# The first expert product released after the first picks, and three half down units queued ahead of the ninth place

## What is computed

```python
def expert_block(args):
    toks, wb, e = args
    xb = hf[toks]
    hid = jax.nn.silu(jnp.matmul(xb, w_g[e])) * jnp.matmul(xb, w_u[e])
    return jnp.matmul(hid, w_d[e]) * wb[:, None]
```

## Time and profile before

| | |
|---|---|
| time, median of 3 runs | 1052.52 us (1051.52 to 1053.54) |
| time of the profiled execution | 1054.09 us |
| its span, first to last instruction | 1051.9 us |
| mean granted TensorE clock | 0.938 of full speed |
| PE busy | 913.0 us (87%) |
| DVE busy | 469.8 us (45%) |
| ACT busy | 345.5 us (33%) |
| read from memory | 298.84 MB |

### The profile page before, as it was taken

The page is one execution under the profiler, slowest core; times in us unless marked ns, Lnnn a source line. Parts: engine busy times, 40 slices in busy tenths (PEclk is TensorE's granted clock), DMA queues, the critical chain, the costliest instruction groups (busy, mean ns, idle before and its releaser), DMA issues.

```text
span 1051.9 us, 14155 instructions
## 1 busy us (share of the span) xinstructions
PE 913.0 (87%) x5968; PEld 661.4 (63%) x5968; DVE 469.8 (45%) x795; ACT 345.5 (33%) x557; POOL 6.1 (1%) x13
## 2 busy tenths in 40 slices
PE   6999999989889865867676775999999989999997
PEld 6969878954236421312222131388999989999986
DVE  6789869411001010010101010189766676888842
ACT  5432465211000010100000010258655745666632
POOL 0000000000000000000000000000100000000000
PEclk9999999999989987888888796999999999999999
DMA  9785332969999999999999999982434244565451
GB/s 319 273 299 205 145 120 90 409 242 426 423 407 426 409 426 425 424 429 424 428 420 429 423 427 426 406 308 82 129 132 161 81 161 160 173 210 180 163 198 40
DMA packets 78331, 301.24 MB, mean 286 GB/s; under 512 B 4035, under 2 KB 30788, under 8 KB 62658
## 3 DMA queue, kind: packets, MB, share of 16 engines
q1 hardware_dynamic: 76624, 298.83, 72.1%
q10 hardware_dynamic: 1314, 1.07, 0.4%
q0 software_dynamic: 336, 0.53, 0.3%
HBM read 298.84 MB, written 1.05 MB: 285 GB/s over the span
## 4 chain that ended last, share of the span: by engine, by line
PE 60%; DMA 28%; DVE 6%; ACT 3%; issue 1%; SPq 1%; DVEq 0%; PEldq 0%; ACTq 0%
PE bank L1406 11%; DMA ring<-in_w_gate_e_dram 9%; DMA ring<-in_w_down_e_dram 8%; DMA ring<-in_w_up_e_dram 7%; PE bank L1068 7%; PE bank L1424 6%; PE bank L682 5%; PE bank L1297 3%; PE bank L1312 3%; PE bank L773 3%; PE bank L1126 3%; PE bank L709 2%; DMA qvpr<-in_w_down_e_dram 2%; PE bank L1098 2%; PE bank L941 2%; PE bank L1201 2%
## 5 line engine op out<-in xcount | busy, mean ns | idle before, releaser
L1068 PE MATMUL bank<-ring,big 128*32 128x512 f32 x768 | 164.2, 714 | 79.2 <-DMA ring<-in_w_up_e_dram 40.3
L1068 PEld LDWEIGHTS bank<-ring,big 128*32 128x32 f32 x768 | 39.3, 127 | 196.0 <-issue 92.7
L349 DVE TENSOR_TENSOR ring_parts<-ring,ring_parts 128x2048 fp32r<-128x2048 f32 (+1 forms) x54 | 118.8, 2248 | 37.6 <-ACT ring_parts L341 37.3
L341 ACT ACTIVATE ring_parts<-ring 128x2048 fp32r<-128x2048 f32 (+1 forms) x54 | 98.5, 1874 | 54.1 <-DMA ring<-in_w_up_dram 27.0
L2244 DVE TENSOR_TENSOR xT<-bank,xT 128x512 f32<-128x512 f32 x32 | 22.1, 692 | 138.5 <-PE bank L1112 138.5
L1406 PE MATMUL bank<-mrg_parts,ring_parts 128*128 128x256 f32 x640 | 82.3, 281 | 0.0
L1406 PEld LDWEIGHTS bank<-mrg_parts,ring_parts 128*128 128x128 f32 x640 | 78.5, 189 | 0.0
L2199 DVE TENSOR_TENSOR big<-big,const 128x128 f32<-128x128 f32 x14 | 3.5, 289 | 157.9 <-PE bank L1055 157.9
L1068 PE MATMUL bank<-hs,big 128*32 128x512 f32 x128 | 67.8, 682 | 0.0
L1098 PE MATMUL bank<-ring,big 128*32 128x512 f32 x336 | 46.9, 687 | 19.1 <-DMA ring<-in_w_down_e_dram 16.3
L1068 PE MATMUL bank<-qvpr,big 128*32 128x512 f32 x112 | 60.7, 695 | 0.6 <-DMA qvpr<-in_w_gate_e_dram 0.6
(11 more groups left out here) (398 smaller groups left out, 1614.6 us busy)
## 6 DMA issues: line engine op xcount, KB each, us to landing
ring<-in_w_up_e_dram SPq DMA_DIRECT2D x24, 2048.0 KB, 28.8
ring<-in_w_gate_e_dram SPq DMA_DIRECT2D x24, 2048.0 KB, 22.3
ring<-in_w_down_e_dram SPq DMA_DIRECT2D x17, 2048.0 KB, 20.7
ring<-in_w_in_dram SPq DMA_DIRECT2D x12, 2048.0 KB, 14.1
ring<-in_w_up_dram SPq DMA_DIRECT2D x22, 1024.0 KB, 7.0
ring<-in_w_down_e_dram SPq DMA_DIRECT2D x12, 1024.0 KB, 20.6
ring<-in_w_down_dram SPq DMA_DIRECT2D x5, 2048.0 KB, 7.8
ring<-in_w_out_dram SPq DMA_DIRECT2D x4, 2048.0 KB, 9.0
```

What stands on the lines that cost most here:

```text
L341: signal(act.activation(pairs[stage][u % 3][0][:, part], raws[stage][u % 3][:, part], ACT.Copy), stage + "_hi")
L349: signal(eng.tensor_tensor(lo[:, part], raws[stage][u % 3][:, part], hi[:, part].bitcast(F32), ALU.subtract), name)
L1068: mm = pe.matmul(bank[part][CAP * j:CAP * j + CAP, :], xeT[:, c, CAP * j:CAP * j + CAP], w[j][c], start=(c == 0), stop=(c == DC - 1))
```

## The change

DVE increments `hidden` and `added` directly behind the first two picks, not behind the number of turns. As the routing scratch and `sig` share words, ACT now waits for `rounds` before it starts `expert_step`. PE no longer waits for the bank of `cnt` ahead of the first expert product; it waits for it before `late_keys`, together with the banks of `kx` 4 and 5. On SP the three first halves of the units 9, 10 and 11 are issued one behind the other, and the wait for `keys_read` with the load of the second half of the ninth place comes after all three. No arithmetic changes.

```diff
                 for i in range(3):
-                    if i == 2:
-                        sp.wait_ge(S["keys_read"], 1)
-                        load_spare(1)
                     sp.wait_ge(S["half_used"], i + 1)
                     w = w_d[0, (i + 1) // 2, (i + 1) % 2]
                     sp.dma_start(expert_slots[i][:, 0:2048], w[:, 0]).then_inc(S["down_early"], 16)
+                sp.wait_ge(S["keys_read"], 1)
+                load_spare(1)
                 sp.wait_ge(S["half_used"], 4)
...
             GATHER_BANKS = (5, 6)
-            late = [("cnt", 0)]
-            assert not any(PLACE[use][0] in GATHER_BANKS for use in late)
+            assert not PLACE[("cnt", 0)][0] in GATHER_BANKS
...
             gather(range(4))
             keys_by_chunks(4, range(6, 8))
-            for use in late:
-                copied(pe, use)
...
                     if part and first and step == 0:
-                        for m_ in (4, 5):
-                            copied(pe, ("kx", m_))
+                        for use in (("kx", 4), ("kx", 5), ("cnt", 0)):
+                            copied(pe, use)
                         late_keys()
...
                 move(("kx", m), att[:, (8 + m) * T:(9 + m) * T], T)
+            act.wait_ge(S["rounds"], 1)
...
                 dve.tensor_tensor(pick[:, t], here, iota, ALU.is_equal).then_inc(S["pick_step"], 1)
+            dve.sem_inc(S["hidden"], 1)
+            dve.sem_inc(S["added"], 1)
...
             last_turn = dve.value_load(count_i[0:1, 0:1], min_val=PAIRS - 1, max_val=PAIRS * ROUNDS - 1)
-            dve.sem_inc(S["hidden"], 1)
-            dve.sem_inc(S["added"], 1)
```

## The result

| | before | changed |
|---|---|---|
| median, 7 runs each | 1052.52 us (1051.20 to 1053.73) | 1047.54 us (1045.58 to 1049.14) |
| ratio of the two | | 0.9946, 95% interval 0.9933 to 0.9959 |
| the same, on another chip, 11 runs of the changed kernel | | 0.9966, 0.9952 to 0.9981 |
| span of the profiled execution | 1051.9 us | 1043.8 us (1044.4 in the second) |

The changed kernel is faster, by 5.0 us in the medians (5.7 us by the ratio, 4.3 to 7.1 by its interval), and by 3.6 us (2.0 to 5.1) on the other chip. The forecast was 5.3 us; the median of the first chip agrees with it, the interval of the second ends just short of it.

A forecast was written before the change was run, and what follows sets the result against it. The expert weight stream was taken to bound the kernel from 231 to 676 us. PE's 2.78 (wait) and 1.69 (clock) give 4.47 us; with the order the stream's lead is 5.3: 1052.5 - 5.3 = 1047.2 us, range 1045.2 to 1049.8.

The forecast's parts named there:

- The word: PE's first expert product, released earlier, starts at 214.05 instead of 216.83: 2.78 us of wait gone.
- the three conditions: What PE's first expert product still waits for: the picks, the rows and PE's own queue, the queue being latest.
- The clock: Without the idle time PE's clock stays up, so the first expert product takes 3.57 us, not 5.26: 1.69 us.
- The order: SP issues three halves before the `keys_read` wait, closing a stream break; the stream's lead becomes 5.3 us against PE's 4.47.
- the break closes: The weight stream's second break, at 228 to 231 us, worth 1.73 us, disappears; not all of it is kept.
- a gap of 0.8 us: New stream gap: the queue ends at 241.6, data of the up product's end trigger start at 242.4.
- "nearly closed": With 0.6 us to the first byte, the new gap would nearly vanish: lead 6.2 us, time 1046.3.
- The covers: Moved waits cost nothing: count's bank has 11.6 us of cover, ACT's `rounds` wait is early, DVE's increments some tenths at most.
- The rival on the other side: Slower: the ninth place lands about 10 us or more after issue, delaying the up product; 1054.8 us, chance 0.04.
- The passage to the end: While the weight stream sets the pace, each microsecond of earlier start is worth one at the end, unless broken anew.
- 15 us of queue: Step 1's first three units, 6.29 MB from 245.51 on; what PE frees meanwhile is issued without a break.
- the later dip at 356 us: Stream dip of 1.2 us at 356 to 364, from late memory keys; moves with the stream, plus or minus 1.2 us.

The follow-up runs named there:

- e5: Kernel before, with 6 unread matmuls of 128x256 filling PE's idle time ahead of the first expert product; ratio 0.9995 (0.9986 to 1.0004).
- e3: Changed kernel, with PE's wait for the count's bank also kept ahead of the first expert product; ratio to the kernel before 0.9967 (0.9956 to 0.9978).
- e4: Kernel before, with 24 unread matmuls of 128x256 put on PE ahead of the first expert product; ratio 1.0058 (1.0041 to 1.0075).
- e2: Kernel before, with only SP's new order of loads, the word still given late; ratio 0.9987 (0.9977 to 0.9998).
- e1: Changed kernel with SP's old order of loads, so only the early word remains; ratio to the kernel before 0.9957 (0.9944 to 0.9970).
- e6: Changed kernel, with 6 unread matmuls ahead of the first expert product to delay it without idle time; ratio to the kernel before 0.9980 (0.9971 to 0.9989).
- g2: Changed kernel with first halves as quarters, step 1's unit 0 in halves, and PE's turn-count read moved early; ratio to the kernel before 0.9952 (0.9935 to 0.9968).
- f2: Changed kernel, with unit 0 of step 1 loaded in two halves, the first at half the up product; ratio to the kernel before 0.9951 (0.9938 to 0.9964).
- g1: Changed kernel, with PE's read of the number of turns moved ahead of the memory's keys; ratio to the kernel before 0.9949 (0.9935 to 0.9964).
- f1: Changed kernel, with the three first half units split into quarters, the first quarters issued earlier; ratio to the kernel before 0.9958 (0.9945 to 0.9971).
- f3: Changed kernel with first half units as quarters and unit 0 of step 1 in two halves; ratio to the kernel before 0.9953 (0.9940 to 0.9966).

## Why the prediction was right, step by step

**The word.** Forecast 2.78 us of wait; the start moved from 3.74 to 0.96 us behind the key chunk, 2.78. That PE's own queue would be the last of the three conditions held. **The clock.** Forecast 1.69; the product took 1.70 us less, and e5 gives 1.59 at the marks with the idle time filled and nothing else changed. That it is the idle time that does it was argued from one case in the prediction; for this place e3, e4 and e5 show it (2.71 us of it: fallen; 1.00, or none: not). It isn't a rule on length: elsewhere the clock fell behind 2.40 us and held behind 2.90 (last section).

**The order.** Forecast: the break closes, a gap of 0.8 us opens behind it, 0.8 us net. Measured: gap 0.47 us, net 1.0 by bytes (e2), and 0.9 to 1.0 between e1 and the changed kernel. The first issue's data started later than in the sum: 115 and 213 GB/s at 218 to 220 put the start at 219.2, 1.73 us behind the issue and not 1.32. The shorter gap made up for it: that the two errors, 0.4 and 0.3 us, cancel is luck. The Trainium skill's 0.6 us to the first byte ("DMA: Bandwidth & Descriptors", section "Latency and other measured facts") would have given a lead of 6.2 us, as the prediction's estimate. The 1.73 us and the lead of 5.3 speak against using it for a stream here. The prediction's "nearly closed" gap takes the 0.6 us for the second restart alone; taken for both, the gap stays 0.8 us, with the same lead.

**The covers.** ACT's new wait, the count's wait ahead of the late keys and DVE's two increments cost nothing that shows: L999 starts 226.41 - 222.84 = 3.57 us behind the product, as before. The ninth place landed 2.5 us before PE asked for it, against 3.5 us in the sum. The rival on the other side had its first condition half fulfilled (7.3 us to land, where 10 would decide), and no more. The Trainium skill's rule on completion out of issue order ("DMA: Bandwidth & Descriptors", section "Queues, rings and completion order") did no harm here. Of the ninth place's 7.3 us, 2.8 are the halves still ahead of it (219.2 + 7.5 - 223.9) and 2.5 its own bytes.

**The passage to the end.** Forecast: one for one. e4 shows it over 5.9 us. But two steps were thinner than I put them. I said that within 15 us of queue what PE frees is issued without a break; behind the next trigger, at 278.86, a gap worth 0.44 us opened all the same. And I said that the later dip at 356 us moves with the stream and is good for plus or minus 1.2 us. The table shows that it decides: in eight of the thirteen rows the lead at the last mark is that of the trigger, within 0.2 us, whatever it was at the first mark (e3: 3.32, 1.81, 1.85; e6: 2.64, 0.96, 0.98). Between them lie 47 us in which PE alone sets the time, and the clock can fall in it at two places, behind the landing of the first mark and at the loop's entry. Their number gives the length of the stretch. In eight profiles the clock fell at one place, and it is 47.5 to 47.6 us. In e1 and g2 it also fell at one place, but ahead of the first product behind the landing, and it is 48.4 and 48.2. In e3, e6 and f2 it fell at both: 49.0 to 49.2. In g1 it fell at neither: 45.8. The profile before and the first one after are both of the first kind (47.52 and 47.56 us), so the 5.4 us came through; that both drew the same kind was luck too. This is a part of the spread of the runs, with the 2.4 us behind the last landing.

**Open.** Why e2, f1, f3, g1 and g2 lose 0.5 to 2.6 us between the trigger and the last mark was not settled. The landings in between narrow it down: from the one near 400 us to the one near 597 us each of these leads keeps within about 0.2 us, and 0.5 to 1.5 us of each are lost from there to the last mark (in f3 1.5 between the landings at 633 and 674 us). The rest, in f3 and g1 above all, is lost between the trigger and 400 us. No run isolates either. And the gain in time itself is known only to 2.0 to 7.1 us over both measurements, so the times can't say which of the last marks' 5.1 to 5.4 us is right, and the second measurement (3.6 us, 2.0 to 5.1) leaves open that less than the forecast reaches the end.

## What to carry to other kernels

A wait that looks like 2.7 us can be worth more: ask what the idle time does to the clock of the work behind it, and what that work releases. A lead in a stream of transfers lives only until the next trigger that the queue doesn't cover; before making a start earlier still, look for the next such trigger (here the end of the up product, then that of the next gate product). Compare executions from a common event next to the edit, and check a mark's scatter on profiles whose code is the same up to it, before reading a difference from it; bytes moved over a stretch were steadier here. After moving a cost away from one place, look for it in the new one (g1). All of this matters when one execution's clock can differ by more than the effect.

## What the runs showed of the hardware

- 1.00 to 1.1 us of idle time on PE left the clock at 1.00 (e3, g1, g2); behind 2.71 us it was at 0.50 to 0.75 from 218 to 222 us (before; e2 likewise). After 1.94 to 1.99 us it fell in five of twelve executions and not in seven, in the same code: at this length it is open which way it goes.
- Longer waits are open too. At the wait for the landing of the first mark it fell behind 2.79 to 5.17 us of idle time in eleven profiles, and held behind 2.81 us (g1), 2.11 (e5) and 1.99 (f1). In f3 and g2, in the same code up to there, it fell to 0.50 behind 2.40 us and stayed at 1.00 behind 2.90 us:

```profile
284.03 8.75 PE L1076 MATMUL bank<-ring,big 128*32 128x512 f32 x58 [2.40 <-DMA ring<-in_w_up_e_dram]
```

```profile
283.50 7.05 PE L1076 MATMUL bank<-ring,big 128*32 128x512 f32 x58 [2.90 <-DMA ring<-in_w_up_e_dram]
```

- The data of a first transfer after a pause started 1.3 to 1.7 us after the issue (1.32 before, 1.73 and 1.64 in two profiles of the changed kernel, 1.65 in e3).
- A float32 matmul of 128x256 took 0.44 us when issued back to back (24 in 10.52 us), and stands in the trace as two records.
- The read of a number into PE's sequencer cost 0.84 to 0.9 us of PE's idle time, directly ahead of a loop as well as ahead of 14 us of matmuls (g1, g2: 1.53 us of idle time ahead of the keys instead of 0.69).
